# TensorE multiplies the matrix of ones with itself ahead of 41 of its steps

## The reference

```
first block:   x += parallel_mixer(rms_norm(x))            # indexer top-k attention (dsa) and latent attention (mla), gated
               x += memory_cross_attention(rms_norm(x))    # "mem0", 4 heads of 64, 256 memory rows
               x += hierarchical_moe(rms_norm(x))          # 16 experts
second block:  x += rms_norm(even_mixer(rms_norm(x)))      # forgetting attention (fox) and sparse attention (nsa)
   layer 0     x += rms_norm(memory_cross_attention_2(rms_norm(x)))   # "mem1"
               x += rms_norm(swiglu(rms_norm(x)))          # "ffn 0"
   layer 1     x += rms_norm(diff_mixer(rms_norm(x)))      # differential attention (diff)
               x += rms_norm(memory_cross_attention_2(rms_norm(x)))   # "mem2"
               x += rms_norm(swiglu(rms_norm(x)))          # "ffn 1"
```

## Time and profile before

| | |
|---|---|
| time, median of 3 runs | 2382.69 us (2381.18 to 2384.85) |
| the profiled execution: span, and its own time | 2384.1 us (nothing is shown outside the span) |
| PE busy | 2205.8 us (93%) |
| DVE, ACT, POOL busy | 1237.1, 1116.8, 717.4 us |
| mean granted clock of TensorE | 0.964 |
| TensorE idle, all waits together | 178.3 us |

### The profile page before, as it was taken

How to read it: one execution, slowest core, us unless ns; L and a number is a source line. 1 busy time by engine, 2 the same in 40 slices (tenths; PEclk the granted TensorE clock), 3 DMA queues, 4 the chain that set the end, 5 groups by cost and what they waited for, 6 DMA issues and landing times.

```text
span 2384.1 us, 29845 instructions
## 1 busy us (share of the span) xinstructions
PE 2205.8 (93%) x10776; PEld 1785.1 (75%) x10776; DVE 1237.1 (52%) x2214; ACT 1116.8 (47%) x1958; POOL 717.4 (30%) x475
## 2 busy tenths in 40 slices
PE   7888899989999999988978999998988888999997
PEld 5655688767888887766857888887877767788886
DVE  6768544547999824455455322224567455323233
ACT  5455733456888725555353322224666334322221
POOL 4160223420000222510333323234742424333223
PEclk9879999999999999988999999999999989999999
DMA  4301032315999720220221233222311221323231
GB/s 163 115 19 36 15 106 97 115 71 196 396 392 386 280 89 19 71 97 1 74 68 57 93 107 96 98 92 67 102 58 36 71 71 40 102 97 98 97 98 53
DMA packets 71649, 258.85 MB, mean 109 GB/s; under 512 B 7952, under 2 KB 8080, under 8 KB 71120
## 3 DMA queue, kind: packets, MB, share of 16 engines
q1 hardware_dynamic: 66816, 238.76, 28.6%
q0 software_dynamic: 2816, 11.82, 1.3%
q10 hardware_dynamic: 1872, 6.37, 0.7%
HBM read 245.36 MB, written 11.56 MB: 108 GB/s over the span
## 4 chain that ended last, share of the span: by engine, by line
PE 79%; DVE 8%; ACT 6%; issue 3%; POOL 2%; DMA 1%; POOLq 0%; DVEq 0%; SPq 0%; ACTq 0%
PE ps L506 16%; PE ps L507 16%; PE ps L508 16%; PE ps L1133 3%; PE ps L566 2%; PE ps L2701 2%; PE ps L2703 2%; PE ps L2702 2%; PE ps L1148 2%; PE ps L542 2%; PE ps L548 2%; PE ps L543 2%; PE ps L1167 2%; PE ps L2728 1%; PE ps L2729 1%
## 5 line engine op out<-in xcount | busy, mean ns | idle before, releaser
L448 ACT ACTIVATE wh<-raw 128x1024 fp32r<-128x1024 f32 x308 | 322.3, 1054 | 454.0 <-PE ps L508 426.8
L453 DVE TENSOR_TENSOR wl<-raw,wh 128x1024 fp32r<-128x1024 f32 x180 | 245.4, 1369 | 532.7 <-ACT wh L448 525.0
L506 PE MATMUL ps<-hh,wh 128*128 128x512 f32 (+1 forms) x1192 | 468.4, 393 | 5.9 <-POOL wl L453 5.6
L507 PE MATMUL ps<-hl,wh 128*128 128x512 f32 (+1 forms) x1192 | 465.7, 391 | 0.0
L508 PE MATMUL ps<-hh,wl 128*128 128x512 f32 (+1 forms) x1192 | 465.4, 390 | 0.0
L453 POOL TENSOR_TENSOR wl<-raw,wh 128x1024 fp32r<-128x1024 f32 x128 | 309.3, 2417 | 473.7 <-ACT wh L448 464.5
L506 PE MATMUL ps<-act,wh 128*128 128x512 f32 (+1 forms) x688 | 270.8, 394 | 11.3 <-ACT act L1408 9.9
L507 PE MATMUL ps<-act,wh 128*128 128x512 f32 (+1 forms) x688 | 268.9, 391 | 0.0
L508 PE MATMUL ps<-act,wl 128*128 128x512 f32 (+1 forms) x688 | 268.6, 390 | 0.0
L506 PEld LDWEIGHTS ps<-hh,wh 128*128 128x128 f32 (+1 forms) x1192 | 224.5, 188 | 54.9 <-issue 7.9
L508 PEld LDWEIGHTS ps<-hh,wl 128*128 128x128 f32 (+1 forms) x1192 | 224.4, 188 | 47.7
(11 more groups left out here) (463 smaller groups left out, 3885.0 us busy)
## 6 DMA issues: line engine op xcount, KB each, us to landing
raw<-d_w SPq DMA_DIRECT2D x277, 512.0 KB, 3.7
raw_x<-d_moe SPq DMA_DIRECT2D x84, 512.0 KB, 6.3
raw<-d_moe SPq DMA_DIRECT2D x84, 512.0 KB, 6.5
d_xs<-Sb POOLq DMA_DIRECT2D x7, 514.0 KB, 7.3
Xb<-d_xs ACTq DMA_DIRECT2D x6, 514.0 KB, 5.5
area<-d_mem POOLq DMA_DIRECT2D x3, 1024.0 KB, 5.1
d_ys<-rows ACTq DMA_DIRECT2D x6, 512.0 KB, 6.0
xT<-d_x SPq DMA_DIRECT2D x8, 256.0 KB, 6.6
```

Of the source, the lines that this page charges most:

```text
L448: me.e.activation(hi, raw, ACT.Copy).then_inc(*me.done("wh", m))
L453: me.e.tensor_tensor(lo, raw, hi.bitcast(F32), ALU.subtract).then_inc(*me.done("wl", m))
L506: me.e.matmul(bank[0:m, 0:n], wh[:, c], hi, start=k == 0, stop=False)
L507: me.e.matmul(bank[0:m, 0:n], wh[:, c], lo, start=False, stop=False)
```

## The change

A new function multiplies the constant matrix of ones (128x128, float32) with itself, some times over, into the first 128 columns of a bank that has just been taken, and on which the next product starts anew (`start=True`), so that what it writes is never read. A table `K.warm` says at which steps and how often. It is called right behind `take`, ahead of the waits for the operands, in `linear`, `linear_group`, `spread_root`, `products_pe`, `turn_pe`, the rotation of mla, the indexer's scores (`rel`), the first part of `hid` and the three forms of diff. No semaphore and no operation of another engine is changed. The table has 41 steps that are reached, with 357 products of the program.

```diff
@@ -488,8 +488,15 @@
     return (K.wh[:, 0, :], K.wl[:, 0, :]) if K.plan.dry else K.halves(tile)
 
 
+def keep_warm(K, me, key, bank):
+
+    for _ in range(K.warm.get(key, 0)):
+        me.e.matmul(bank[:, 0:128], K.ones, K.ones, start=True, stop=True)
+
+
 def linear(K, me, key, name, layer, columns, src, m=128, n=T, row0=0, after=None, pool="ps"):
     bank = K.banks[me.take(pool, *key)]
+    keep_warm(K, me, key, bank)
     for k, (hi, lo, ready) in enumerate(src):
         b = block(K, me, lo is not None, (name, layer, row0 + 128 * k, columns))
         tile, c = b // 8, slice(b % 8 * 128, b % 8 * 128 + m)
@@ -522,6 +529,8 @@
 
 def linear_group(K, me, specs, src, norm=None):
     banks = [K.banks[me.take("ps", *key)] for key, *_ in specs]
+    if specs:
+        keep_warm(K, me, ("group", specs[0][0][1]), banks[0])
     for k, (hi, lo, ready) in enumerate(src):
         first, last = k == 0, k == len(src) - 1
         if norm and last:
@@ -1121,6 +1131,7 @@
 def products_pe(K, me, a, p, pair):
     it = pair[0]
     score_banks(K, me, it, (a, p))
+    keep_warm(K, me, (a, "products", p), K.bank("S", a, p, 0, 0))
     for h in range(2):
         for k in pair[h]["tok"]:
             me.wait_ge(*k)
@@ -1140,6 +1151,8 @@
     for h in range(2):
         for pk, pack in enumerate(packs(it)):
             bank = K.banks[me.take("ps", "T", a, p, h, pk)]
+            if h == 0 and pk == 0:
+                keep_warm(K, me, (a, "turn", p), bank)
             for i in range(NQ):
                 me.wait_ge("exp", a, p, h, i)
             for j, i0, c0 in pack:
...
@@ -3239,6 +3254,8 @@
                 if l0 == 0:
                     me.take("ps", "hid", s)
                 bank = K.bank("hid", s)
+                if l0 == 0:
+                    keep_warm(K, me, ("hid", s), bank)
                 for l in range(l0, l0 + 8):
                     b = block(K, me, False, ("cmp_w1", s, l, None))
                     tile, end = b // 8, padded(K, b) and not K.plan.dry
...
@@ -3511,6 +3528,7 @@
 
 def diff_products_pe(K, me, n, it):
     score_banks(K, me, it, ("diff", n))
+    keep_warm(K, me, ("diff", "products", n), K.bank("S", "diff", n, 0, 0))
     for k in it["tok"]:
         me.wait_ge(*k)
     for i, part in score_order(it):
...
@@ -3811,6 +3832,16 @@
     K.group_after = {"x4": ("L", ("mq", "mem1"), 0), "x7": ("L", ("mq", "mem2"), 0), "x3": ("L", "fqk", 0), "x5": ("gl", ("ffn", 0), 0, 0), ("ffn", 0): ("L", "dqk", 0), "x8": ("gl", ("ffn", 1), 0, 0)}
     K.next_norm = {("ffn", 0): "n6", ("ffn", 1): None}
     K.before = {("ffn", 0): ("x", "x5"), ("ffn", 1): ("x", "x8")}
+    K.warm = {("group", ("mq", "mem1")): 12, ("group", ("mq", "mem2")): 12, ("group", ("ffn", 0)): 10, ("group", ("ffn", 1)): 10,
+              ("group", "dqk"): 10, ("rot", "mlar"): 14, ("hid", 0): 14, ("hid", 1): 14, ("feat", 7): 14, ("diff", "products", 0): 12,
+              ("diff", "turn", 7): 8, ("bc", "n1"): 8, ("bc", "n4"): 6, ("bc", "n7"): 6, ("fox", "products", 0): 6,
+              ("nsa", "products", 0): 7, ("nsa", "turn", 0): 4, ("res", "x2", 0): 9, ("sw", "x5", 0): 9, ("sw", "x8", 0): 9,
+              ("sw", "x4", 0): 14}
+    for m in ("mem0", "mem1", "mem2"):
+        K.warm.update({(("matt", m), "products", 0): 10 if m != "mem0" else 0, (("matt", m), "products", 1): 6, (("matt", m), "turn", 0): 7})
+    K.warm.update({("rel", 1, 0): 6, ("rel", 1, 2): 9, ("rel", 1, 4): 9, ("rel", 1, 6): 8, ("bc", ("lat", 0)): 14,
+                   ("bc", ("lat", 2)): 4, ("dsa", "products", 0): 8, ("dsa", "turn", 0): 4})
+    K.warm.update({("mla_att", "turn", p): n for p, n in enumerate((16, 4, 4, 4))})
     K.o_last = [None] * 4
     order = ["n0", "n1", "n2", "n3", ("y", "x4"), "n4", ("y", "x5"), "n5", ("y", ("ffn", 0)), "n6", ("y", "x7"), "n7",
              ("y", "x8"), "n8", ("y", ("ffn", 1))]
```

More of the change, by code:

```diff
@@ L1532, in latent_pe @@
     bank = K.banks[me.take("ps", "rot", "mlar", 0)]
+    keep_warm(K, me, ("rot", "mlar"), bank)
     me.wait_ge("xh", "mlar", 0)
@@ L1756, in mixer_pe @@
             bank = K.banks[me.take("ps", "rel", i, n)]
+            keep_warm(K, me, ("rel", i, n), bank)
             me.wait_ge("tok", "idx", 1)
@@ L3529, in diff_turn_pe @@
         bank = K.banks[me.take("turns", "T", "diff", n, pk)]
+        if pk == 0:
+            keep_warm(K, me, ("diff", "turn", n), bank)
         me.wait_ge(*normed)
@@ L3634, in diff_features_pe @@
     bank = K.banks[me.take("turns", "feat", m)]
+    keep_warm(K, me, ("feat", m), bank)
     me.wait_ge("scaled", m)
```

## The result

The changed kernel took 2400.68 us (median of four runs, 2391.45 to 2401.8) beside 2383.77 of the kernel before in the same series: 1.006 times the time before [1.0039, 1.0082], so slower by 14.3 us by this ratio and by 16.9 us by the two medians. I had forecast 2376.0 with 2392 as the upper end. The execution that was profiled is the fastest of the four (2391.45, span 2389.5), 5.4 us above the profiled one of before, so the profile shows the smaller part of the loss.

The account below looks back on a forecast made before the run. TensorE, busy in 93% of the span, was taken to bound the kernel, the low clock costing 69.7 us. Cost 23.1 less gain 29.7 gave -6.6 us, from the median 2382.69 to 2376; range 2362 to 2392.

Parts of the forecast that it names:

- rival C: Products of ones do not hold the clock at all; 23 to 31 us are paid: 2409; chance 0.05.
- rival D: Low clock costs less than half of busy time; the 14 stretches give 12 of 35.7 us: +11, 2394; chance 0.04.
- which steps are filled and which not: At 23 of 41 steps (213 products) an operand's wait hides the ones; at the other 18 (144 products) not.
- the wait for L929: In mem1, for DVE's event that frees the bank: stays, now ahead of L494, score products 2.1 us behind it.
- B: Clock falls again soon after; 17.8 us gained, 23 to 26 us paid: +5 to +8 us, 2389; chance 0.27.
- I take five sixths, 29.7 us: Gain from the low-clock stretches behind the 23 operand-wait steps: 29.7 us of at most 35.7.
- I take 0: Memory attentions' turns, 21 products, 4.5 us: a 1.60 us wait after 12 transposes takes up 1.5; cost taken as 0.
- The 50 score products: In mem0, mem1, mem2 and diff: ones run after the bank's wait and delay the scores, 10.7 us, ends 0 and 13.
- The 43 products without a wait: First scores of dsa, fox, nsa, root of n1, second `hid`: cost 9.2 us, 5 if later waits take it up.
- First `hid` with nsa's turn: 14 and 4 products, 3.8 us of ones, partly taken up by short waits for DVE's maximum; cost 1.7 us.
- The turns of dsa and diff: Turns of dsa (4 products) and diff 7 (8): 2.6 us, short waits take 1.1, cost 1.5 us.
- 0.213: Assumed us per product of ones (two instructions of 128 columns) in rows of many; all 357 are 76 us.

Follow-up runs that it names:

- e4_wide: The change with ones only ahead of the event: 23 operand-wait steps, moved score products, further waits filled, 12 steps dropped; 2354.03 us, 0.9875 of the kernel before.
- e1_filled: The change with ones only at the 23 steps (213 products) where the wait is for an operand; 2373.37 us, 0.9962 of the kernel before.
- e2_rest: The change with ones only at the other 18 steps (144 products), behind the wait or without one; 2414.47 us, 1.0128 of the kernel before.
- e7_no_turns: The change without the 21 products ahead of the memory attentions' turns; 2390.06 us, 1.0029 of the kernel before.

## Why the prediction was wrong

**Right.** That products of ones hold the clock (rival C fell: 139.40 to 65.16 us of work at the low clock). That work at the low clock costs half of its busy time where TensorE is the limit (rival D fell: with its third, 12 of 35.7, the 52.1 us that e4_wide took away would be worth 17.5 at most, and it is 29.1 faster). The Trainium skill's page "TensorE: Matmul & The Clock Gate" puts the loss to the ramp under 1% of a typical span (Part 1, "What's actually happening"); the 29.1 us measured here are 1.2% of this kernel's time, and that is the gain alone, so for this kernel the measurement decides against that figure. Right too was which steps are filled and which not (but for x4, where the low clock made the ones outlast the wait by 1.1 us), and that the wait for L929 would stay in mem1 with the score products behind the ones.

**The step that failed: the sum of gain and cost, on both sides, the gain above all.** Forecast were -29.7 and +23.1; measured were -10.9 (e1_filled) and +30.2 (e2_rest), by the medians. Of the rivals, B is nearest: slower, and part of the gain lost because the clock falls again. But by the medians it lost more than B's half, only part of it that way, and the cost was above B's 23 to 26.

- "I take five sixths, 29.7 us". e1_filled, which has nothing but these steps, gives 10.9 in the median and 18.1 in its profile. I had kept back 6.0 us; the runs keep back 18 to 25. One part is that the clock falls again at waits left empty (231.7, 2020.3): 28.2 us in place of 35.7. The other is the 10.1 us in the profile that the clock gives and the span does not show. I took every busy microsecond of the stretches as one that the end waits for. The indexer's 2.35 us were not: its loop has the same length at both levels. Some 4 us more came back as longer waits, half of them for DVE's `hl` (4.0 us for 2.0); that TensorE would catch up with DVE was among my reasons for the sixth, at too low a price. For the other 4 us the place is open.
- "I take 0" for the memory attentions' turns. 4.7 us in the profile of the change by the delays there (1.6, 1.7 and 1.4), 6.7 by e7_no_turns. That the exponential "itself comes later" was in the text, but for the wrong cause, and I did not follow ACT's queue back from it to the turn.
- The 50 score products, 10.7: in the profile the score products start later by 1.5, 2.4, 2.2, 2.6, 4.0 and 2.1, together 14.8. The price was wrong (0.24), and mem2's ten met the low clock (4.0). In the 2.2 and 2.1 only 1.5 each are ones; the rest is that the bank's wait grew from 1.22 and 1.19 to 2.06 us, as the products ahead of it were no longer at the low clock.
- The 43 products without a wait, 9.2: 2.1, 3.6, 1.4, 1.6 and 3.1, together 11.8. Most of the excess is n1 (3.6 for eight, at the low clock).
- First `hid` with nsa's turn, 1.7: 3.3 and 1.0, of which 2.1 are taken up by the next waits, 2.2. The turns of dsa and diff, 1.5: 0.8 in all, as a wait of 1.62 us takes up diff's.
- Together 34.3 for 23.1; e2_rest says 27.4 in its profile and 30.2 in the median. The ends that I gave the sum, 13 and 31, do not come out of its items either: their lower ends add up to 8.2 and their upper ones to 29.9.
- "0.213" came from column sums, 24 in a row at 0.108, and from one row at the low clock. The ones cost 0.237 to 0.25: 14 in 3.32 us at 1013.30, ten in 2.40 at 1229.19, six in 1.51 at 1235.64. By these three an instruction takes about 0.113 us and each block some 0.15 more, an estimate.

With the measured terms, 30.2 - 10.9 is +19.3, within 6 us of what the change measured (13.6 and 16.9). The mechanism of the forecast was right in its two halves, a clock that is held and ones that come late. What failed is the sum: two large terms of opposite sign, the cost came out nearly a third above what I had given it and the gain at little more than a third, and that turned the sign. My own observable for B, over 120 us of low stretches, was no good test: they were 71.60 and 85.50 us and the kernel was slower all the same.

## What to carry to other kernels

Filler work pays only where it is issued ahead of the event that ends the wait, and that holds for the wait for a bank as for that for an operand: take a bank that is free early, multiply, and wait then. Before a later wait is trusted to take up a delay, follow the queue of the engine that ends it back; if it runs through the delayed work, nothing is taken up. A stretch at the low clock is worth half of its busy time only where nothing else sets its pace and no wait for another engine follows that takes the gain up, and if some waits are filled, the empty ones beside them become the next places where the clock falls.

## What the runs showed of the hardware

- A wait of the same length (2.14 us ahead of the root at 241.37 in the kernel before and at 232.65 in e1_filled) was followed by the high clock in one kernel and by the low one in another, though TensorE's instructions are the same from 17 us ahead of it.
- Two executions of one program differ in their low clock: 65.16 and 81.61 us of TensorE's work in the change, 82.97 and 96.12 in e1_filled. With it the spans differ by 6.4 and 9.5 us. That is as much as whole experiments here are worth (e7_no_turns 6.7, e1_filled 10.9), and a reason to compare medians over many runs.
- With few low stretches left the runs lie closer together: 2353.14 to 2356.48 in e4_wide, but these are four runs only; in each of the other changed kernels the runs span over 9 us.
- A float32 product of 128 columns, two instructions, cost 0.24 us within the program and 0.45 at the low clock (476.53).
- Six products of 512 columns took 5.18 us at the low clock and 2.82 at the high one, and the wait for ACT behind them grew from 1.28 to 4.63 us: the gain was gone at the next wait.
